# Scan stage of a hybrid diffusion step: inverse levels on all four 64x64 quadrants of TensorE, a reordered chain step, and products moved to GpSimd

## The reference, cut to what matters

```
def step(S, inp):                      # one token of one head; S is 64x64
    r_t, w_t, k_t, v_t, a_t, b_t = inp
    sa = S @ a_t
    S = S * w_t + outer(sa, b_t) + outer(v_t, k_t)
    return S, S @ r_t
bonus = sum over channels and directions of r * k_dir * r_k      # per token and head, times v
```

## Time and profile before

| what | value |
|---|---|
| median of 2 runs | 3531.68 us (3530.76 to 3532.59) |
| the profiled execution | 3528.82 us, its span 3527.2 us |
| PE busy in the span | 3135.8 us (89%) |
| the scan stage, about 2212 to 3313 us | 16 rounds |
| one round, taken as the sample | 2641.53 to 2710.61 us |

### The profile page before, as it was taken

The page is one execution under the profiler, slowest core; times in us unless marked ns, Lnnn a source line. Parts: engine busy times, 40 slices in busy tenths (PEclk is TensorE's granted clock), DMA queues, the critical chain, the costliest instruction groups (busy, mean ns, idle before and its releaser), DMA issues. The chain is left out here.

```text
span 3527.2 us, 75367 instructions
## 1 busy us (share of the span) xinstructions
PE 3135.8 (89%) x33458; PEld 1996.9 (57%) x33458; DVE 1568.1 (44%) x2748; ACT 694.3 (20%) x1312; POOL 260.3 (7%) x360
## 2 busy tenths in 40 slices
PE   7499999979888896859999997899999999999689
PEld 1155555533434443425554443888888888888534
DVE  0222222226676662131000002667766777676476
ACT  0212222110000000120000011333333333333111
POOL 0000000000000000000000000121111112111100
PEclk9799999979888898979999998999999999999889
DMA  6222222231111004103233231100010001000252
GB/s 249 97 87 89 85 85 85 84 123 33 48 51 51 30 30 186 50 24 92 88 104 115 86 110 37 30 21 21 21 39 21 21 21 39 21 21 22 98 208 78
DMA packets 198171, 247.18 MB, mean 70 GB/s; under 512 B 38339, under 2 KB 145363, under 8 KB 195460
## 3 DMA queue, kind: packets, MB, share of 16 engines
q1 hardware_dynamic: 182904, 192.12, 16.8%
q0 software_dynamic: 14992, 50.87, 3.7%
HBM read 189.45 MB, written 53.49 MB: 69 GB/s over the span
## 5 line engine op out<-in xcount | busy, mean ns | idle before, releaser
L104 PE MATMUL ps<-hT,hw 128*128 128x512 f32 (+1 forms) x2048 | 560.8, 435 | 6.2 <-DMA hw<-in_hy_w_in 6.2
L104 PEld LDWEIGHTS ps<-hT,hw 128*128 128x128 f32 x2048 | 312.4, 191 | 252.0 <-issue 252.0
L104 PE MATMUL ps<-mix,rw 128*128 128x512 f32 (+1 forms) x1024 | 283.0, 440 | 11.0 <-DMA rw<-in_rw_w_k 5.7
L104 PE MATMUL ps<-rwv,mix 128*128 128x512 f32 x640 | 274.9, 592 | 0.8 <-ACT rout L118 0.8
L104 PEld LDWEIGHTS ps<-mix,rw 128*128 128x128 f32 x1024 | 157.3, 194 | 136.8 <-issue 136.8
L104 PEld LDWEIGHTS ps<-rwv,mix 128*128 128x128 f32 x640 | 121.5, 190 | 153.6 <-issue 152.6
L107 DVE SCALAR_TENSOR_TENSOR mix<-xx,col,hT 128x640 f32<-128x640 f32 x48 | 38.6, 879 | 287.6 <-PE ps L104 287.5
L112 DVE TENSOR_SCALAR hcv<-hpad,hpc 128x641 f32<-128x641 f32 x48 | 29.6, 616 | 305.0 <-ACT hpad L118 305.0
L104 PE MATMUL ps<-e_decays,e_bk 64*64 64x128 f32 x2560 | 162.9, 274 | 0.0
L118 ACT ACT_TABLE_LOAD x70 | 89.8, 1283 | 340.9 <-PE ps L104 235.3
L1478 POOL TENSOR_TENSOR CTm<-CT,tab 128x384 f32<-128x384 f32 (+1 forms) x160 | 133.7, 862 | 283.8 <-ACT CT L118 163.5
(11 more groups left out here) (223 smaller groups left out, 4790.3 us busy)
## 6 DMA issues: line engine op xcount, KB each, us to landing
hw<-in_hy_w_in SPq DMA_DIRECT2D x64, 512.0 KB, 4.1
aw<-in_ada_w SPq DMA_DIRECT2D x16, 1536.0 KB, 7.8
scratch_vx_d<-hot POOLq DMA_DIRECT2D x32, 320.0 KB, 2.8
scratch_rk_d<-rout POOLq DMA_DIRECT2D x32, 320.0 KB, 3.5
scratch_vz_d<-rtok POOLq DMA_DIRECT2D x40, 256.0 KB, 2.3
rw<-in_rw_w_r SPq DMA_DIRECT2D x16, 512.0 KB, 4.0
rw<-in_rw_w_k SPq DMA_DIRECT2D x16, 512.0 KB, 4.1
rwv<-in_rw_w_v SPq DMA_DIRECT2D x4, 2048.0 KB, 9.9
```

Of the source, the lines that this page charges most:

```text
L104: return nc.tensor.matmul(out, lhsT, rhs, start=first, stop=last)
```

## The change

- The chunks are grouped by parity (`CHUNKS`). Even chunks stay on the two diagonal quadrants of the array; odd chunks use the other two (rows 0 to 63 with columns 64 to 127, and the reverse) in `T` and `Y`, and come back in `Z`. The function `quarters` issues even and odd chunks alternately; each level step then has one semaphore step for all 10 chunks.
- Two turns move from EARLY to LATE, and `FILLS` puts 2, 2, 4 and 1 jobs into levels 1 to 4. Of the prep steps on PE, one is placed after `Z` of level 4, one before `Z` of level 5, three after the levels, and the rest in chain steps 2 and 6 and at the end.
- In a chain step the product of `BKT` and `V` moves behind `U`, and the output terms are put in two places (2 terms, then up to 6) where there were three.
- The bonus products `kr` and the products of `e1` with `r` go from DVE to POOL, behind its five levels of `CTm`; SP's load of `r`, PE's bonus step and the next round's scores wait for POOL.

```diff
-    CHUNKS = [slice(0, 6), slice(6, NC)]
+    CHUNKS = [slice(g, NC, 2) for g in range(2)]
-    EARLY = [("bk", g) for g in range(4)]
-    LATE = [("Mk", g) for g in SIDE_ORDER] + [("bk", 4)]
+    EARLY = [("bk", g) for g in range(2)]
+    LATE = [("Mk", g) for g in SIDE_ORDER] + [("bk", g) for g in range(2, 5)]
+    FILLS = {1: (1, 1), 2: (1, 1), 3: (2, 2), 4: (1, 0)}
...
+                    po.wait_ge(prep["dve"].sem, prep["dve"].now(("kd", 0), j))
+                    link(gp.tensor_scalar(kr[:, :], kd[:, 0, :], pcl[:, 6:7], None, MUL))
+                    po.wait_ge(prep["dve"].sem, prep["dve"].now(("kd", 1), j))
+                    link(gp.tensor_scalar(kr1[:, :], kd[:, 1, :], pcl[:, 7:8], None, MUL))
+                    link(gp.tensor_tensor(kr[:, :], kr[:, :], kr1[:, :], ADD))
+                    po.wait_ge(s_l["r"], j * 16 + 16)
+                    link(gp.tensor_tensor(kr[:, :], kr[:, :], r[:, :], MUL), "krr")
+                    for d in range(2):
+                        po.wait_ge(prep["dve"].sem, prep["dve"].now(("pcd", d), j))
+                        pp.did(gp.tensor_tensor(e1[:, d, :], e1[:, d, :], r[:, :], MUL), ("r", d))
...
+                    def quarters(banks, lhsT, rhs, turned_in):
+                        for n in range(NG):
+                            for g in range(2):
+                                for h in range(2):
+                                    src, dst = HALVES[h], HALVES[h ^ g]
+                                    if turned_in:
+                                        src, dst = dst, src
+                                    last = mm(ps[dst, banks[g], n * C:(n + 1) * C], lhsT[src, 2 * n + g, :], ident[src, src] if rhs is None else rhs[src, 2 * n + g, :], n == 0, n == NG - 1)
+                        return last
...
-                            main["pe"].did(each(cs, T_BANK[g], lambda c: F[:, c, :], lambda c: eye), ("T", lv, g))
-                        fill(1)
+                        main["pe"].did(quarters(T_BANK, F, None, False), ("T", lv))
+                        fill(before)
...
+                        main["pe"].did(quarters(Y_BANK, CTm[:, lv % 2], M1, False), ("Y", lv))
+                        fill(behind)
+                        if lv == 5:
                             next(later, None)
...
+                        main["pe"].did(quarters(Z_BANK, M2T, Ysb, True), ("Z", lv))
+                        if lv == 4:
...
                             next(later, None)
+                    for _ in range(3):
+                        next(later, None)
...
-                        for q in on:
-                            s, d, m, c = chains[q]
-                            both(slot_of(S_BANK, q), BKT[:, unit(d, c), 1, :], V[:, c, :], False, False)
                         if n:
-                            o_terms(2 * n, 3)
+                            o_terms(3 * n, 2)
...
                         main["pe"].did(last, ("U", n))
+                        for q in on:
+                            s, d, m, c = chains[q]
+                            both(slot_of(S_BANK, q), BKT[:, unit(d, c), 1, :], V[:, c, :], False, False)
...
-                        o_terms(2 * n + 1, 4)
-                        if n in (0, 2, 5):
+                        if n in (2, 6):
                             next(later, None)
+                            o_terms(3 * n + 2, 1)
+                        else:
+                            o_terms(3 * n + 2, 6)
...
                     for lv in range(1, LEVELS):
+                        wait(main["pe"], ("T", lv), i)
...
+                        if lv == 5:
+                            next(later, None)
+                        wait(main["pe"], ("Z", lv), i)
```

More of the change, by code:

```diff
@@ L1528, in prep_steps @@
                     yield
-                    wait(prep["dve"], "krr", j)
+                    wait(prep["pool"], "krr", j)
                     for t in range(NT):
@@ L1581, in body @@
                     wait(prep["dve"], "ar", i)
+                    wait(prep["pool"], ("r", 1), i)
                     for g in SIDE_ORDER:
@@ L1595, in body @@
                         turn(job[1], n % 2)
[L1597 to L1600, removed]
-                        return last
[L1603 to L1606, removed]
+                    for g, cs in enumerate(CHUNKS):
+                        owner(EARLY[g])
+                        D_("C")
+                        for n, c in enumerate(range(g, NC, 2)):
+                            last = both(ps[:, g, n * C:(n + 1) * C], C_[:, c, :], eye, n == 0, n == NG - 1)
+                        main["pe"].did(last, ("CT", g))
+                    def quarters(banks, lhsT, rhs, turned_in):
[6 more added lines that the diff above has]
+                                    last = mm(ps[dst, banks[g], n * C:(n + 1) * C], lhsT[src, 2 * n + g, :], ident[src, src] if rhs is None else rhs[src, 2 * n + g, :], n == 0, n == NG - 1)
+                        return last
                     for lv in range(1, LEVELS):
-                        for g, cs in enumerate(CHUNKS):
+                        before, behind = FILLS.get(lv, (0, 0))
+                        for g in range(2):
                             D_(("F", lv, g))
@@ L1767, in body @@
                         wait(main["pe"], ("CT", g), i)
-                        md.did(act(flat(CT[:, cs, :]), ps[:, g, 0:(cs.stop - cs.start) * C], ACT.Copy), ("CT", g))
+                        md.did(act(CT[:, cs, :], rows(ps[:, g, 0:NG * C]), ACT.Copy), ("CT", g))
                     next(later, None)
+                    turns = [job for job in LATE if job[0] == "bk"]
                     for lv in range(1, LEVELS):
                         for g, cs in enumerate(CHUNKS):
[L1772 to L1775, removed]
+                            wait(main["pe"], ("Y", lv), i)
+                            md.did(act(Ysb[:, cs, :], rows(ps[:, Y_BANK[g], 0:NG * C]), ACT.Copy), ("Y", lv, g))
+                        for _ in range({3: 2, 4: 1}.get(lv, 0)):
+                            job = turns.pop(0)
+                            turned(job, LATE_BANK[job])
                         if lv >= 4:
                             next(later, None)
-                            next(later, None)
+                    next(later, None)
+                    next(later, None)
                     for n, chains in enumerate(STEPS):
@@ L1889, in body @@
                     v_.wait_ge(md.sem, md.here(i))
+                    md.did(tt(C_[:, :, :], Nm[:, 0:NC, :], Nm[:, NC:NU, :], ADD), "C")
+                    v_.wait_ge(md.sem, md.here(i))
+                    md.did(tt(F[:, :, :], C_[:, :, :], spread(between[:, 0, :], C)(NC), MUL))
+                    v_.wait_ge(md.sem, md.here(i))
                     for g, cs in enumerate(CHUNKS):
[L1891 to L1898, removed]
+                        md.did(tt(F[:, cs, :], F[:, cs, :], spread(stk, C)(NG), ADD), ("F", 1, g))
                     def pick(lv, g):
@@ L1927, in body @@
                         fill({1: 2, 2: 2, 3: 2}.get(lv, 0))
+                        if lv == 5:
+                            next(later, None)
+                        wait(main["pe"], ("Z", lv), i)
                         for g, cs in enumerate(CHUNKS):
-                            wait(main["pe"], ("Z", lv, g), i)
-                            md.did(tt(F[:, cs, :], F[:, cs, :], rows(ps[:, Z_BANK[g], 0:(cs.stop - cs.start) * C]), ADD), ("F", lv + 1, g))
-                            if lv + 1 < LEVELS:
+                            md.did(tt(F[:, cs, :], F[:, cs, :], rows(ps[:, Z_BANK[g], 0:NG * C]), ADD), ("F", lv + 1, g))
@@ L1932, in body @@
+                        if lv + 1 < LEVELS:
+                            for g in range(2):
                                 pick(lv + 1, g)
-                        if lv == 4:
-                            next(later, None)
-                            next(later, None)
                     for n, (d, g) in enumerate(((0, 0), (1, 1), (0, 1), (1, 0))):
                         v_.wait_ge(md.sem, md.now(("F", LEVELS, g), i))
-                        us = slice(d * NC + CHUNKS[g].start, d * NC + CHUNKS[g].stop)
```

69 lines of the change are left out of this document (36 added, 33 removed).

## The result

The changed kernel takes 3650.18 us (two runs, 3648.22 to 3652.14) against 3531.68: a ratio of 1.0336, 95% interval 1.0291 to 1.038. The profiled execution has a span of 3646.6 us. The forecast of 3506 us is missed, with the wrong sign and outside its range of 3465 to 3590. That the second rival named 3658 us is a coincidence: its mechanism is not there, as the rows show.

A forecast was written before the change was run, and what follows sets the result against it. The scan was taken as bound by PE, with small latency gaps. Per round 2.0 - 0.1 + 1.15 - 1.5 = 1.55 us less, 25 us in 16 rounds: 3531.7 - 25 = 3506 us, range 3465 to 3590.

The forecast's parts named there:

- second rival: Levels: quadrants don't run side by side, a step still issues in 1.16 us; 126 us slower, 3658 us, chance 0.22.
- 8.7 us of PE time a round: Levels: PE time saved, 15 x 0.58 us; the rest was counted as latency laid bare, leaving 2.0 us less a round.
- The pace of the quadrants: Level steps: four quadrants load abreast, so a step of 40 records issues in 0.58 us instead of 1.16.
- The levels: Levels 1 to 5 up to the chain: 29.6 us a round against 30.45 plus 1.17, so 2.0 us less.
- The start: Start of a round: grows by 0.1 us, since the moved turns were not on its path.
- The chain steps: Chain steps 0 to 7: 26.85 us a round against 28.0, so 1.15 less, with PE waiting for the bonus.
- the order's 1.15: Chain steps: the saving a round forecast with the new order of products and output terms, 1.15 us.
- GpSimd: Moved bonus work: products of 640 columns 1.54 us each, scaling 1.0; meetings with VectorE cost 1.5 us a round.
- the full price of 3.0: GpSimd beside VectorE: cost a round if each meeting blocks, 3.0 us; bounds 0 and 3.0, half (1.5) taken.
- the 67.5 forecast: Whole round: about 67.5 us instead of 69.1.
- The rival on GpSimd as harmless: Moved products: GpSimd and VectorE don't disturb each other; 49 us saved, 3483 us, chance 0.22.
- the one on the quadrants: The second rival: level quadrants don't run side by side, 9.45 us a round lost there; 3658 us, chance 0.22.

The follow-up runs named there:

- e3: The changed kernel plus seven matmuls, whose results nobody reads, on TensorE just before its wait for the bonus products: 3604.05 us, 1.0206 to the kernel before.
- e7: The kernel of e1 with four turns of the next chunk's work in front of the levels again, instead of two: 3527.27 us, 0.9991 to the kernel before.
- e5: The kernel of e1 with all level products on the two diagonal quadrants, so the inverse comes out wrong: 3663.07 us, 1.0381 to the kernel before.
- e10: The kernel of e7 with products nobody reads put into TensorE's waits in the levels: 3513.54 us, 0.9938 to the kernel before.
- e9: The kernel of e3 with more products nobody reads, ahead of T and Z in the levels: 3609.07 us, 1.022 to the kernel before.
- e1: The changed kernel with the bonus and r products back on VectorE: 3566.41 us, 1.0096 to the kernel before.
- e4: The changed kernel with GpSimd's two scalings by a column written as products with that column broadcast: 3636.58 us, 1.0297 to the kernel before.
- e6: The kernel of e1 with the old order of the chain step, BKT products ahead of U and output terms in three places: 3581.53 us, 1.0144.
- e2: The kernel before with only the bonus and r products moved to GpSimd: 3558.91 us, 1.0074 to the kernel before.
- e12: The kernel of e8 with products nobody reads ahead of T of levels 2 to 5 and Z of level 5: 3474.96 us, 0.9822 to the kernel before.
- e8: The kernel of e7 with its own turns, scores and prep products reordered into TensorE's waits in the levels: 3461.54 us, 0.9816 to the kernel before.

## Why the prediction was wrong

- **The step that failed** is the one that turned 8.7 us of PE time a round into latency and had the waits cost only their length. A clock that moves was in none of its cases. A us at 1.2 GHz costs 0.38 by e3, 0.40 by e7's two rounds, 0.46 by e5's levels ((40.5 - 37.92) / 5.6); with 16.8 us more of them in a round than before that is 6.4 to 7.7 us, some 100 to 125 in all. e3, which keeps the wait and loses the slow stretch, shows it for the wait for the bonus. For the levels e7 and e10 support it, less cleanly, since their slow rounds also have stalls or added work; e9 has 3.2 us less at 1.2 GHz than e3 and is no faster. The Trainium skill, "TensorE: Matmul & The Clock Gate", HAM oscillation — how this bites in real kernels, describes an engine that waits between groups and starts the next at half clock; the traces agree (0.50 behind a wait of 3.07 us).
- **The pace of the quadrants** was right: 0.60 us for a forecast 0.58.
- **The levels** were forecast at 29.6 us. In five kernels with this order (the change, e1, e3, e4, e6) a line through 75 rounds, length of the levels against their time at 1.2 GHz, gives 30.1 at full clock. No such round is free of low clock, so this is an estimate; the sample round, 32.01 less 0.38 to 0.46 for each of its 3.8 us, gives 30.3 to 30.6. That is a gain of 1.0 to 1.5, not 2.0. The waits of 1.1 and 0.97 us are those named.
- **The start** was to grow by 0.1; without low clock it goes from 9.64 (12 rounds) to 10.38 (7 of e1). The two turns moved were no longer cover for VectorE's chain; in e7 it is 9.72.
- **The chain steps** were forecast at 26.85, with a wait of about 1.1 for the bonus in it. e5, without GpSimd's part and without that wait, has 21.34 to the bonus and 4.80 behind it at full clock, 26.1: near the forecast less its wait. e6 finds one us of the order's 1.15.
- **GpSimd** was mis-sized, by its meetings with VectorE. Its sum and product take 1.53 us, as estimated, where VectorE has no product of two SBUF tiles of 640 columns beside them, and about 2.1 beside one. Its scaling takes 1.88 beside one, 2.44 or 2.51 beside two and 3.08 or 3.16 beside three: some 0.6 for each. No run has it alone, so whether the 1.0 was right stays open. So products do meet, but it is mostly GpSimd's instruction that grows; of VectorE's products of 0.82, which were to take 1.5, one a round takes 1.17. The wait for the bonus is 3.07 us in the sample and 3.2 us of stage length in the table (25.81 against 22.61): the full price of 3.0 that the text held as its bound, not the half that it took.
- **Together**: 10.38 + 30.1 + 21.34 + 3.2 + 4.80 = 69.8 us a round at full clock. Against the 67.5 forecast that is 2.3 us, 37 us in 16 rounds: 3543 us, inside the range. The 107 us from there to 3650 are 6.7 a round, and the 16.8 us more at 1.2 GHz make 6.4 to 7.7. The rival on GpSimd as harmless falls by e2, the one on the quadrants by e5.

What stays open is why the low clock comes in the later levels and the chain steps: e5 and e12, whose PE has more to do in the levels, keep most of it or all, and e8 still has two rounds with some 17 us at 1.2 GHz beside eleven of 15 with none in their levels. Nor is it known how the 84 us of GpSimd's part divide exactly (e3 gives back 46 with the wait left in place), where the stalls put down to issue come from (7.9 us in the scan of the change, 0.8 before), and whether filled waits would help as much without the quadrants: no run fills them in the kernel before.

## What to carry over

Halving an engine's work where it hid the hand-overs between the others lays these bare, and on TensorE here such a wait was paid twice: as a wait and as slow work behind it. So after such a change put the kernel's own loose work into the new waits, as e8 did, before judging the change. Price the windows with the granted clock beside them, and a move to another engine by what will stand beside each instruction there.

## What the hardware showed

- Two rounds with the same instructions took 65.9 and 76.2 us, at a mean granted clock of 0.97 and 0.87; a prep product took 1.34 us in the one and 2.50 in the other.
- Added products in a wait of 3 us made the changed kernel 46 us faster (e3).
- GpSimd's scaling of 128x640 by a column took 1.88 us beside one VectorE product of two SBUF tiles of that size, 2.51 beside two and 3.16 beside three; its own product of two such tiles 1.53 beside none and 2.07 beside one. VectorE's scaling took 0.55.
- Four 64x64 quadrants took 40 records in 0.60 us, two in 1.18.
